# Decay matrices of a chunked gated DeltaNet: from masked triangle matmuls to cumulative sums spread by DMA, GpSimd adds and ScalarE exponentials

## The chip, the cores and the metric

One Trainium2 chip, one core. The metric is the device time of the whole kernel in microseconds (us), the median of several runs. A profiled execution has a span (first to last instruction) and a time of its own a little above it. Engines: PE is TensorE (PEld its weight loads), DVE is VectorE, ACT is ScalarE, POOL is GpSimd, SP is SyncE, which here only issues DMAs.

## The reference, cut to what matters

One layer over 512 latent tokens and 256 context tokens, width 2048: RMSNorm with adaLN, one combined input projection, a bidirectional gated DeltaNet (8 heads of 128), a grouped-query attention, gates, and output projections. Everything is float32. The change touches only the preparation of the DeltaNet, whose chunked form is:

```python
gcum = jnp.cumsum(gc, axis=-1)                       # log decays g <= 0, per token, head, direction
diff = gcum[..., :, None] - gcum[..., None, :]
decay_incl = where(incl, exp(diff), 0)               # incl: i >= j; strict: i > j
l_mat = (k*beta) @ k.T * decay_strict                # then (I + L)^-1 [v*beta, k*beta*exp(gcum)]
attn_intra = q @ k.T * decay_incl
q_dec, k_dec = q*exp(gcum), k*exp(gcum_last - gcum)
o = q_dec @ S + attn_intra @ v_new;  S = S*exp(gcum_last) + k_dec.T @ v_new
```

The kernel works with chunks of 128 tokens (the result doesn't depend on the chunk), so for each token tile, head and direction it needs a 128x128 matrix of decays.

## The kernel before, in words

**Weights.** Every big matmul is float32 made from three float32r products (`three`, L1675-1680): hi*hi, hi*lo, lo*hi. The weights come in 297 pieces of up to 128x1024 elements. For each piece SP loads `w_raw` (L561, two buffers), ACT rounds it to `w_hi` (`hi_part`, L766), DVE subtracts to get `w_lo` (`lo_part`, L1105), and PE multiplies. `w_hi` and `w_lo` have two buffers each. Each engine runs one loop over piece numbers n in program order. In iteration n, ACT first makes `w_hi` of piece n+1, which waits until PE has used piece n-1, and DVE first makes `w_lo` of piece n+1. So `w_lo` of piece n+1 has to be finished between the start and the end of PE's work on piece n.

**Slots.** The gate projections are pieces 121 to 216, of four k-tiles each. A k-tile is six 128x512 matmuls. Behind each k-tile PE, ACT and DVE run whatever `scan_plan` (L104) has put at that place, called a slot below; four slots make a piece. Slot number kk belongs to piece 122 + kk//4.

- Slots 0 to 119 prepare twelve *units* (L112-119). A unit is one token tile and one half of the heads (4 heads), both directions d. Units 0 to 3 are context tiles, at slots 0, 8, 16, 24; units 4 to 11 are latent tiles, at slots 32, 43, 54, 65, 76, 87, 98, 109. Relative to the unit's first slot: `kt` at +0, `decay` +1, `gram` +2, `qk` +3 (latent only), `lower` +5, `upper` +7, `at` +9 (latent only).
- From slot 126 the *scan* runs twelve pairs of units, each a chain of slots `couple5`, `ks`, `correct5`, `qs`, `couple6`, `correct6`, `z`, `az`, `kz`.
- The output of a gate group goes to DRAM in the first and the third slot of every fourth piece, with a Silu or Sigmoid on ACT (`gate_stage`, L1029). These need another table than the Exp of the `decay` slot.

**A unit, before.** `kt`: PE transposes four key blocks (L1693), ACT scales them into `k_rows` (L832, eight 128x128). `decay`: POOL has written masked copies of the log decays, high and low float32r parts (`decay_rhs`, L600, four 128x512); PE multiplies them by a triangle (L1702, L1703, two per direction); ACT takes Exp of PSUM into `decay` (`DD`, L842, one 128x512 per direction). `gram`: PE makes k.kT (L1710); DVE multiplies by a token factor and `decay` into `L` (L1215, eight 128x128). `lower` and `upper`: DVE copies out diagonal blocks (L1197, four 32x128 each, L1200 a transpose), and SP stores them (L518). `qk`: PE makes q.kT (L1715), DVE multiplies it into `decay` (L1225), POOL masks the result (`mask_scores`, L608). `at`: PE transposes that (L1721, eight), ACT copies it to `scoresT` (L848, two 128x512), SP stores it at +10 (L523).

**POOL** also inverts 32x32 diagonal blocks (`block_steps`, L627, L631), four steps of it in each latent unit, and loads and stores them by DMA. SP loads for the scan (L477, L485) after the last blocks are stored; the first scan matmul (L1760) waits for `L`.

Of the kernel before, what the change touches and what calls it, by code (L numbers as in the profile page):

```python
# [7 lines left out]
P = 128  # L8
# [11 lines left out]
NT = LT + CT  # L20
# [12 lines left out]
NCONST = SEL + 8  # L33

# [69 lines left out]
def scan_plan():  # L104
# [41 lines left out]
def build(nc, x, c, ctx, c_ctx, w_mod, b_mod, norm_w, w_in, conv_w, a_log, dt_bias, a_norm_w, q_norm_w,  # L146
# [80 lines left out]
    tri_r = [at(f"triangle{d}", [P, P], A_MASKS + 512 * d, f32r) for d in (0, 1)]  # L227
# [70 lines left out]
    GMH = [at(f"decay_rhs_hi{d}", [P, 4, P], A_C + 12288 + 2048 * d, f32r) for d in (0, 1)]  # L298
    GML = [at(f"decay_rhs_lo{d}", [P, 4, P], A_C + 16384 + 2048 * d, f32r) for d in (0, 1)]
    DD = [at(f"decay{d}", [P, 4, P], A_C + 20480 + 2048 * d) for d in (0, 1)]  # L300
# [11 lines left out]
    g_hi = at("g_hi", [P, NT * 16], A_T + 12288, f32r)  # L312
    g_lo = at("g_lo", [P, NT * 16], A_T + 12672, f32r)
# [48 lines left out]
    kr_scr = nc.dram_tensor("k_rows_scratch", [N_UNITS, P, 2, 512], f32, kind="Internal").ap()  # L362
    block_in = nc.dram_tensor("block_in_scratch", [N_UNITS, 8, P, 32], f32, kind="Internal").ap()
    block_out = nc.dram_tensor("block_out_scratch", [N_UNITS, 8, P, 32], f32, kind="Internal").ap()

    with ExitStack() as stack:
# [101 lines left out]
        def _(sp):  # L468
# [36 lines left out]
            def scan_transfers(kk):  # L505

                for u in UNITS:
# [67 lines left out]
        def _(pool):  # L575
# [13 lines left out]
            pool.wait_ge(S("prep"), 1)  # L589
            pool.wait_ge(S("w_used"), N_GATE0)  # L590
            def decay_rhs(u):
                for d in (0, 1):

                    col = unit_col(d, u["tile"], 4 * u["half"])
                    m = (GT, LT_)[d]
                    mask = consts[:, m:m + P].unsqueeze(1).to_broadcast([P, 4, P])
                    if u["i"]:
                        pool.wait_ge(S("decay_mm"), 2 * u["i"])
                    for part_t, g_t in ((GMH, g_hi), (GML, g_lo)):
                        ins = pool.tensor_tensor(part_t[d][:], mask,  # L600
                                                 g_t[:, col:col + 4].bitcast(f32).unsqueeze(2).to_broadcast([P, 4, P]), ALU.mult)
                    ins.then_inc(S("decay_rhs"), 1)

            def mask_scores(u):
                for d in (0, 1):
                    m = (GE, LE)[d]
                    pool.wait_ge(S("decayed"), 2 * u["li"] + d + 1)
                    pool.tensor_tensor(DD[d][:], DD[d][:], consts[:, m:m + P].unsqueeze(1).to_broadcast([P, 4, P]),  # L608
                                       ALU.mult).then_inc(S("masked"), 1)
# [31 lines left out]
            decay_rhs(UNITS[0])  # L641
            pool.memset(X64[:], 0.0).then_inc(S("zeroed"), 1)
            pool.wait_ge(S("kv_spill"), 16 * NT)
            pool.memset(SS[:], 0.0).then_inc(S("zeroed"), 1)
            for u in UNITS:
                if u["i"] + 1 < N_UNITS:
                    decay_rhs(UNITS[u["i"] + 1])
                if u["lat"]:
                    mask_scores(u)
                    if u["li"] == 0:  # L650
                        blocks_load(0)
                    block_steps(1 + 4 * u["li"], min(31, 5 + 4 * u["li"]))
            blocks_store(0)
            for d in (0, 1):
                pool.wait_ge(S("decay_mm"), 2 * N_UNITS)
# [94 lines left out]
        def _(act):  # L750
# [71 lines left out]
            def prepare(slot):  # L822
# [12 lines left out]
                elif k == "decay":  # L835
                    for d in (0, 1):
                        act.wait_ge(S("decay_mm"), 2 * i + d + 1)
                        if i:
                            act.wait_ge(S("L"), 2 * i)
                        if u["li"]:  # L840
                            act.wait_ge(S("scoresT_mm"), 2 * u["li"])
                        act.activation(DD[d][:], bank4(4 + 2 * d), ACT.Exp).then_inc(S("decay"), 1)  # L842
                elif k == "at":
                    for d in (0, 1):
                        act.wait_ge(S("scoresT_mm"), 2 * u["li"] + d + 1)
# [73 lines left out]
            for n in range(N_PA0):  # L919
# [62 lines left out]
                if n == GROUPS[G_BKV]["first"] + 5:  # L982

                    act.wait_ge(S("ab_rows"), 1)
                    ab = bank(6, NT * 32).rearrange("p (t c) -> p t c", t=NT)
                    act.activation(beta[:].rearrange("p (t c) -> p t c", t=NT), ab[:, :, 0:16], ACT.Sigmoid).then_inc(
                        S("beta"), 1)
                    act.wait_ge(S("negabs"), 1)
# [3 lines left out]
                    act.activation(alog[:], alog[:], ACT.Exp).then_inc(S("ab_exp"), 1)  # L992
                    act.wait_ge(S("ssq_eps"), 1)
                    ln(act.activation(rk[:], rk[:], ACT.Sqrt))
                    act.activation(rq[:], rq[:], ACT.Sqrt).then_inc(S("ssq_std"), 1)
                if n == GROUPS[G_BKV]["first"] + 6:
                    act.wait_ge(S("cum"), 1)
                    act.activation(DEC[:].rearrange("p a b c -> p (a b c)"), bank(6, NT * 2 * 24), ACT.Exp).then_inc(
                        S("decays"), 1)
                if n == N_GATE0:  # L1000
                    g = GROUPS[G_BKV]
                    for t in range(NT):
                        if t == 0:
# [88 lines left out]
        def _(dve):  # L1092
# [18 lines left out]
            for d, m in enumerate((LE, GE)):  # L1111
                dve.tensor_copy(tri_r[d][:], consts[:, m:m + P]).then_inc(S("triangles"), 1)
# [90 lines left out]
            def prepare(slot):  # L1203
# [31 lines left out]
            def scan(slot):  # L1235
# [5 lines left out]
                for d in (0, 1):  # L1241
# [44 lines left out]
                    elif k == "az":  # L1286
                        o = o_acc[:, tile, 4 * half * P:(4 * half + 4) * P].rearrange("p (u n) -> p u n", u=4)
                        dve.tensor_tensor(o, ps, o, ALU.add).then_inc(done, 1)
# [120 lines left out]
            for n in range(N_PA0):  # L1409
# [57 lines left out]
                if n == GROUPS[G_BKV]["first"] + 5:  # L1467
                    dve.wait_ge(S("ab_rows"), 1)
                    dve.wait_ge(S("beta"), 1)
# [7 lines left out]
                    dve.tensor_tensor(ab_t[1][:], ab_t[0][:], ab_t[1][:], ALU.min).then_inc(S("negabs"), 1)  # L1477
                    dve.wait_ge(S("ab_exp"), 1)
# [10 lines left out]
                    dve.scalar_tensor_tensor(out=v3(gdec), in0=v3(ab_t[0]), scalar=-1.0,  # L1489
                                             in1=alog[:].unsqueeze(1).to_broadcast([P, NT, 16]),  # L1490
                                             op0=ALU.mult, op1=ALU.mult).then_inc(S("g_ready"), 1)
# [3 lines left out]
                    dve.tensor_scalar(rq[:], bank(7, 32, 48), EPS, None, ALU.add).then_inc(S("ssq_eps"), 1)  # L1495
                    dve.wait_ge(S("ssq_std"), 1)
# [7 lines left out]
                if n == GROUPS[G_BKV]["first"] + 7:  # L1504
                    dve.wait_ge(S("decays"), 1)
                    ln(dve.tensor_scalar(ngr[:].rearrange("p (a h) -> p a h", h=8), DEC[:, :, 0, :], -1.0, None, ALU.mult))
                    ln(dve.tensor_tensor(v4(ngr), v4(ngr), rkb, ALU.mult))
                    ln(dve.tensor_copy(g_hi[:], gdec[:]))
# [543 lines left out]
```

## Time and profile before

| what | value |
|---|---|
| median of 3 runs | 1830.5 us (1828.3 to 1832.72) |
| profiled execution, own time | 1831.48 us |
| its span | 1828.9 us |
| PE busy | 1765.8 us, 97% |
| PEld busy | 1449.0 us, 79% |
| DVE busy | 946.3 us, 52% |
| ACT busy | 661.7 us, 36% |
| POOL busy | 277.3 us, 15% |
| mean granted TensorE clock | 0.993 |

The shares are over the whole span. The units' slots run from about 558 us to 765 us, the scan from 777 us to 1102 us. In the lines of the trace the first number is the start in us, the second the length, xN the number of instructions merged; square brackets give the idle time of that engine just before and what ended it.

### The profile page before, as it was taken

What the parts mean: (1) busy time and instruction counts of PE and PEld (TensorE: products, weight loads), DVE (VectorE), ACT (ScalarE), POOL (GpSimd) and SP (SyncE); (2) the same over time, 40 slices, a digit from 0 to 9 for tenths busy, and PEclk for the clock granted to TensorE, in tenths of its full rate; (3) what the DMA queues carried; (4) which work ended last, traced back from release to release, by engine and by line L of the source; (5) the groups of instructions that cost most, each with busy time, mean ns of one, the idle gap of its engine ahead of it and who ended that gap; (6) DMA issues with size and microseconds to landing.
All of it is one profiled execution on the core that took longest, in us unless ns stands there. A gap on an engine that the chain in (4) does not pass through costs nothing.

```text
span 1828.9 us, 25605 instructions
## 1 busy us (share of the span) xinstructions
PE 1765.8 (97%) x10286; PEld 1449.0 (79%) x10286; DVE 946.3 (52%) x1662; ACT 661.7 (36%) x1212; POOL 277.3 (15%) x421
## 2 busy tenths in 40 slices
PE   5899999999999999999999999999998999999999
PEld 3568888888787888788888888877877788788887
DVE  2335444365324575545556554764368866453334
ACT  5323321233135546444343435522346444232121
POOL 1000000000004466477000003211101110210000
PEclk9999999999999999999999999999999999999999
DMA  9982222223225666744444437767533333662332
GB/s 370 337 283 58 58 58 58 58 81 86 70 58 179 195 183 187 218 132 144 132 122 139 123 96 227 223 202 208 172 104 98 99 100 97 254 195 92 123 119 104
DMA packets 198685, 267.13 MB, mean 146 GB/s; under 512 B 37072, under 2 KB 135625, under 8 KB 197161
## 3 DMA queue, kind: packets, MB, share of 16 engines
q1 hardware_dynamic: 174944, 192.63, 34.8%
q0 software_dynamic: 15552, 58.62, 9.4%
q10 hardware_dynamic: 8073, 14.27, 2.1%
q8 instruction: 81, 1.33, 0.3%
q14 instruction: 35, 0.29, 0.0%
HBM read 221.96 MB, written 43.52 MB: 145 GB/s over the span
## 4 chain that ended last, share of the span: by engine, by line
PE 82%; DVE 7%; ACT 4%; DMA 4%; issue 2%; POOL 1%; SPq 0%; ACTq 0%; DVEq 0%; POOLq 0%
PE psum L1678 24%; PE psum L1680 23%; PE psum L1679 23%; DMA w_raw_mod<-w_mod_dram 2%; DVE w_lo L1105 1%; PE psum L1789 1%; PE psum L1787 1%; PE psum L1838 1%; PE psum L1671 1%; ACT w_hi L766 1%; PE psum L1793 1%; PE psum L1791 1%; PE psum L1795 1%; DMA w_raw<-w_proj_b_dram 1%; PE psum L2020 1%
## 5 line engine op out<-in xcount | busy, mean ns | idle before, releaser
L1105 DVE TENSOR_TENSOR w_lo<-w_raw,w_hi 128x1024 fp32r<-128x1024 f32 x232 | 290.7, 1253 | 538.9 <-ACT w_hi L766 538.5
L766 ACT ACTIVATE w_hi<-w_raw 128x1024 fp32r<-128x1024 f32 x232 | 245.7, 1059 | 834.2 <-PE psum L1680 776.5
L1678 PE MATMUL psum<-h_hi,w_hi 128*128 128x512 f32 x1152 | 470.7, 409 | 12.5 <-DVE hc_lo L1159 5.6
L1680 PE MATMUL psum<-h_hi,w_lo 128*128 128x512 f32 x1152 | 452.4, 393 | 0.0
L1679 PE MATMUL psum<-h_lo,w_hi 128*128 128x512 f32 x1152 | 451.9, 392 | 0.0
L1678 PEld LDWEIGHTS psum<-h_hi,w_hi 128*128 128x128 f32 x1152 | 217.5, 189 | 71.7 <-issue 23.9
L1680 PEld LDWEIGHTS psum<-h_hi,w_lo 128*128 128x128 f32 x1152 | 217.2, 189 | 48.8
L1679 PEld LDWEIGHTS psum<-h_lo,w_hi 128*128 128x128 f32 x1152 | 218.0, 189 | 36.5
L1174 DVE SCALAR_TENSOR_TENSOR conv_acc<-conv_in,convw,conv_acc 128x772 f32<-128x772 f32 x96 | 98.2, 1023 | 3.4
L1678 PE MATMUL psum<-w_hi,m_hi 128*128 128x512 f32 x256 | 99.6, 389 | 0.0
L1679 PE MATMUL psum<-w_lo,m_hi 128*128 128x512 f32 x256 | 99.6, 389 | 0.0
L1680 PE MATMUL psum<-w_hi,m_lo 128*128 128x512 f32 x256 | 99.6, 389 | 0.0
L600 POOL TENSOR_TENSOR decay_rhs_hi<-consts,g_hi 128x512 fp32r<-128x512 f32 x24 | 27.0, 1124 | 466.6 <-PE psum L1680 406.8
L1678 PE MATMUL psum<-w_hi,h_hi 128*128 128x512 f32 x192 | 75.4, 393 | 2.5 <-ACT gate_stage L1029 1.3
L1680 PE MATMUL psum<-w_hi,h_lo 128*128 128x512 f32 x192 | 74.8, 389 | 0.0
L1679 PE MATMUL psum<-w_lo,h_hi 128*128 128x512 f32 x192 | 74.7, 389 | 0.0
L1678 PE MATMUL psum<-hc_hi,w_hi 128*128 128x256 f32 x256 | 72.6, 283 | 0.0
L1679 PE MATMUL psum<-hc_lo,w_hi 128*128 128x256 f32 x256 | 72.3, 283 | 0.0
L1680 PE MATMUL psum<-hc_hi,w_lo 128*128 128x256 f32 x256 | 72.2, 282 | 0.0
L1678 PEld LDWEIGHTS psum<-w_hi,m_hi 128*128 128x128 f32 x256 | 48.1, 188 | 10.0
L1679 PEld LDWEIGHTS psum<-w_lo,m_hi 128*128 128x128 f32 x256 | 48.1, 188 | 10.0
L1680 PEld LDWEIGHTS psum<-w_hi,m_lo 128*128 128x128 f32 x256 | 48.1, 188 | 9.8
(323 smaller groups left out, 2831.7 us busy)
## 6 DMA issues: line engine op xcount, KB each, us to landing
w_raw<-w_in_dram SPq DMA_DIRECT2D x168, 512.0 KB, 4.0
w_raw_mod<-w_mod_dram SPq DMA_DIRECT2D x64, 512.0 KB, 6.0
w_raw_modg<-w_mod_dram POOLq DMA_DIRECT2D x32, 512.0 KB, 4.5
w_raw<-w_out_dram SPq DMA_DIRECT2D x32, 512.0 KB, 3.7
gate_scratch<-gate_stage ACTq DMA_DIRECT2D x48, 256.0 KB, 4.2
w_raw<-w_proj_a_dram SPq DMA_DIRECT2D x16, 512.0 KB, 4.0
w_raw<-w_proj_b_dram SPq DMA_DIRECT2D x16, 512.0 KB, 3.5
gates<-gate_scratch POOLq DMA_DIRECT2D x32, 256.0 KB, 4.0
```

What stands on the lines that cost most here:

```text
L600: ins = pool.tensor_tensor(part_t[d][:], mask, g_t[:, col:col + 4].bitcast(f32).unsqueeze(2).to_broadcast([P, 4, P]), ALU.mult)
L766: act.activation(part(whi[i % 2], p), part(place, p), ACT.Copy).then_inc(S("w_hi"), 1)
L1105: dve.tensor_tensor(part(wlo[i % 2], p), part(raw_of(n)[0], p), part(whi[i % 2], p).bitcast(f32), ALU.subtract).then_inc(S("w_lo"), 1)
L1174: ins = dve.scalar_tensor_tensor(out=a[:], in0=r[:, tap:tap + 772], scalar=w, in1=a[:], op0=ALU.mult, op1=ALU.add)
L1671: ins = pe.matmul(bank(7, 1, off + t * 8 + it["head"]), a[:, a0:a0 + P], ones[:, 0:1], start=True, stop=True)
L1678: pe.matmul(out_ap, lh, rh, start=first, stop=False, skip_group_check=shared)
L1679: pe.matmul(out_ap, lh, rl, start=False, stop=False, skip_group_check=shared)
L1680: return pe.matmul(out_ap, ll, rh, start=False, stop=last, skip_group_check=shared)
L1787: ins = pe.matmul(ps[:, u, :], kT_of(h, tile), SS[:, d, h, :], start=True, stop=True)
L1789: ins = pe.matmul(ps[:, u, :], YY[d][:, u, :], RR[d][:, u, :], start=True, stop=True)
L1791: ins = pe.matmul(ps[:, u, :], qT[:, h, tile * P:(tile + 1) * P], SS[:, d, h, :], start=True, stop=True)
L1793: ins = pe.matmul(ps[:, u, :], AT[:, d, u, :], ZZ[d][:, u, :], start=True, stop=True)
```

## The change

The decay matrices are no longer made by PE.

1. In the last piece before the gates (`prep`), PE makes cumulative sums of the log decays in two parts: DVE splits each log decay into a multiple of a quarter (adding and taking away `QUARTERS`) and a rest. The sum of the first part, `gdec`, is exact; the exponential of the sum of the rests is a token factor `alpha`. `gdec` is transposed by PE, copied to `cumT` and stored by POOL to DRAM.
2. For each unit POOL issues two DMAs (`cum_load`) that spread four rows of it to all 128 partitions (`CR`, two buffers), and adds a triangle of 0 and 1e30 (`beyond`) to them: `decay_args`, two 128x512 adds, and for latent units two 128x512 subtractions for the transposed matrix.
3. ACT takes Exp of them with the token's sum as bias: one instruction per head and direction, eight of 128x128 into `DD`, and for latent units eight more straight into `scoresT` (`AT`).
4. The scores are made transposed (k.qT), so DVE multiplies them straight into `scoresT` in the `qk` slot. The `at` slot, the mask on POOL and the PE transposes go. SP stores `scoresT` at +6.
5. `alpha` is folded into token factors; in `az` DVE uses it as a scalar: four 128x128 instructions per direction in place of one 128x512.
6. POOL's clearing of `states` moves behind the units.

```diff
-            for m, k in ((0, "kt"), (1, "decay"), (2, "gram"), (5, "lower"), (7, "upper"), (3, "qk"), (9, "at"))[:7 if lat else 5]:
+            for m, k in ((0, "kt"), (1, "decay"), (2, "gram"), (5, "lower"), (7, "upper"), (3, "qk"))[:6 if lat else 5]:
...
-                    if u["lat"] and kk == u["at"] + 10:
+                    if u["lat"] and kk == u["at"] + 6:
...
-            def decay_rhs(u):
...
-                    for part_t, g_t in ((GMH, g_hi), (GML, g_lo)):
-                        ins = pool.tensor_tensor(part_t[d][:], mask, ...)
-            def mask_scores(u):
...
+            def cum_load(u):
+                if u["i"] == 1:
+                    pool.wait_ge(S("kv_spill"), 16 * NT)
+                if u["i"] >= 2:
+                    pool.wait_ge(S("decay_args"), args_of[u["i"] - 2])
                 for d in (0, 1):
+                    r0 = unit_col(d, u["tile"], 4 * u["half"])
+                    pool.dma_start(CR[u["i"] % 2][:, d]..., cum_scr[r0:r0 + 4]....partition_broadcast(P)).then_inc(...)
+            def decay_args(u):
+                pool.wait_ge(S(f"cum_in{u['i'] % 2}"), 32 * (u["i"] // 2 + 1))
+                if u["i"]:
+                    pool.wait_ge(S("L"), 2 * u["i"])
                 for d in (0, 1):
+                    pool.tensor_tensor(DD[d][:], CR[u["i"] % 2][:, d], beyond[d]..., ALU.add).then_inc(S("decay_args"), 1)
+                if not u["lat"]:
+                    return
+                if u["li"]:
+                    pool.wait_ge(S("decayT"), 2 * u["li"])
+                for d in (0, 1):
+                    pool.tensor_tensor(DT[d][:], CR[u["i"] % 2][:, d], beyond[1 - d]..., ALU.subtract).then_inc(S("decay_args"), 1)
...
                 elif k == "decay":                                   # ACT
                     for d in (0, 1):
-                        act.wait_ge(S("decay_mm"), 2 * i + d + 1)
-                        act.activation(DD[d][:], bank4(4 + 2 * d), ACT.Exp).then_inc(S("decay"), 1)
-                elif k == "at":
-                        act.activation(AT[:, d], bank4(4 + 2 * d), ACT.Copy).then_inc(S("scoresT"), 1)
+                        act.wait_ge(S("decay_args"), first + d + 1)
+                        for w in range(4):
+                            ins = act.activation(DD[d][:, w, :], DD[d][:, w, :], ACT.Exp, scale=-1.0, bias=gdec[:, col:col + 1])
+                        ins.then_inc(S("decay"), 1)
+                    if not u["lat"]:
+                        return
                     for d in (0, 1):
+                        act.wait_ge(S("decay_args"), first + d + 3)
+                        if u["li"]:
+                            act.wait_ge(S("scores_out"), 16 * u["li"])
+                        for w in range(4):
+                            ins = act.activation(AT[:, d, w, :], DT[d][:, w, :], ACT.Exp, bias=cum_neg[:, col:col + 1])
+                        ins.then_inc(S("decayT"), 1)
...
-                        dve.wait_ge(S("L"), 2 * i + d + 1)
-                        dve.tensor_tensor(DD[d][:], bank4(7), DD[d][:], ALU.mult).then_inc(S("decayed"), 1)
+                        dve.wait_ge(S("decayT"), 2 * u["li"] + d + 1)
+                        dve.tensor_tensor(AT[:, d], bank4(4), AT[:, d], ALU.mult).then_inc(S("scoresT"), 1)
...
                     elif k == "az":
-                        dve.tensor_tensor(o, ps, o, ALU.add).then_inc(done, 1)
+                        for u in range(4):
+                            ins = dve.scalar_tensor_tensor(out=o, in0=ps[:, u, :], scalar=alpha[:, col:col + 1], in1=o,
+                                                           op0=ALU.mult, op1=ALU.add)
+                        ins.then_inc(done, 1)
...
-                elif k == "decay":                                   # PE
-                        pe.matmul(bank4(4 + 2 * d), tri_r[d][:], GMH[d][:], start=True, stop=False)
-                        pe.matmul(bank4(4 + 2 * d), tri_r[d][:], GML[d][:], start=False, stop=True).then_inc(S("decay_mm"), 1)
...
-                elif k == "at":
-                        for w in range(4):
-                            ins = pe.transpose(bank4(4 + 2 * d)[:, w, :], DD[d][:, w, :], ident)
...
                     for d in (0, 1):
+                        for v in (0, 1):
+                            pe.matmul(split[:, v, :, d, :], consts[:, (LE, GE)[d]:(LE, GE)[d] + P], part_logs, start=True, stop=True)
...
+                    pe.wait_ge(S("prep"), 4)
+                    pe.transpose(bank(7, P, 128)[0:NT * 16], gdec[:], ident).then_inc(S("prep_mm"), 1)
```

## Rows read from the trace of the kernel before

**Rows 1.** Windows: busy us (instructions) of each engine, clock, DMA share, GB/s.

```profile
560.00:760.00 200.00, 199.47 (x1006) 167.60 (x1005) 124.78 (x242) 104.85 (x189) 104.30 (x120) 1.00 0.61 184
```

**Rows 2.** Waits of PE, 500 to 800 us: in total, times, longest.

```profile
PE psum L1760 <- DMA L<-L_scratch: 3.7, 1, 3.7
PE psum L1678 <- ACT kv_stage L1007: 2.2, 1, 2.2
```

**Rows 3.** Timeline of PE in `prep` and in the decay and at slots.

```profile
538.95 1.43 PE L1951 MATMUL psum<-gdec,consts 128*128 128x48 f32 x12
...
559.64 0.39 PE L1702 MATMUL psum<-decay_rhs_hi,triangle 128*128 128x512 f32 x1
...
560.58 0.39 PE L1678 MATMUL psum<-h_hi,w_hi 128*128 128x512 f32 x1
...
626.19 1.03 PE L1721 MATMUL psum<-consts,decay 128*128 128x128 f32 x8
...
626.98 0.48 PE L1678 MATMUL psum<-h_hi,w_hi 128*128 128x512 f32 x1
```

**Rows 4.** Timeline of ACT in the scan: 128x128 instructions from SBUF.

```profile
816.63 2.45 ACT L878 ACTIVATE invT<-invT,beta 128x128 f32<-128x128 f32 x8 [4.24 <-DVE invT L1258]
```

**Rows 5.** Timeline of ACT around unit 8 (slots 76 to 86).

```profile
686.39 1.06 ACT L766 ACTIVATE w_hi<-w_raw 128x1024 fp32r<-128x1024 f32 x1 [0.81 <-PE psum L1680]
688.15 2.17 ACT L832 ACTIVATE k_rows<-psum,decays 128x128 f32<-128x128 f32 x8 [0.69 <-PE psum L1693]
...
693.99 1.08 ACT L842 ACTIVATE decay<-psum 128x512 f32<-128x512 f32 x2
...
697.44 1.06 ACT L766 ACTIVATE w_hi<-w_raw 128x1024 fp32r<-128x1024 f32 x1 [0.46 <-ACT gate_stage L1029]
700.52 1.06 ACT L766 ACTIVATE w_hi<-w_raw 128x1024 fp32r<-128x1024 f32 x1 [2.02 <-PE psum L1680]
```

**Rows 6.** Timeline of DVE around the same unit.

```profile
698.53 1.35 DVE L1105 TENSOR_TENSOR w_lo<-w_raw,w_hi 128x1024 fp32r<-128x1024 f32 x1 [0.51 <-ACT w_hi L766]
```

**Rows 7.** Timeline of ACT and DVE around unit 6 (slots 54 to 64).

```profile
644.21 1.06 ACT L766 ACTIVATE w_hi<-w_raw 128x1024 fp32r<-128x1024 f32 x1 [4.38 <-PE psum L1680]
...
654.05 1.06 ACT L766 ACTIVATE w_hi<-w_raw 128x1024 fp32r<-128x1024 f32 x1
659.25 1.06 ACT L766 ACTIVATE w_hi<-w_raw 128x1024 fp32r<-128x1024 f32 x1 [4.13 <-PE psum L1680]
...
655.15 2.00 DVE L1105 TENSOR_TENSOR w_lo<-w_raw,w_hi 128x1024 fp32r<-128x1024 f32 x1 [7.37 <-ACT w_hi L766]
657.07 2.15 DVE L1215 SCALAR_TENSOR_TENSOR L<-psum,crow,decay 128x128 f32<-128x128 f32 x8
660.34 3.54 DVE L1197 TENSOR_TENSOR L_diagonal<-L,consts 32x128 f32<-32x128 f32 x4
663.89 1.58 DVE L1105 TENSOR_TENSOR w_lo<-w_raw,w_hi 128x1024 fp32r<-128x1024 f32 x1
```

**Rows 8.** Timeline of DVE in a context unit.

```profile
579.94 1.17 DVE L1197 TENSOR_TENSOR L_diagonal<-L,consts 32x128 f32<-32x128 f32 x4
```

**Rows 9.** Lines of POOL, 545 to 766 us: busy, mean ns, idle before.

```profile
L600 POOL TENSOR_TENSOR decay_rhs_hi<-consts,g_hi 128x512 fp32r<-128x512 f32 x24 | 27.0, 1124 | 466.6 <-PE psum L1680 406.8 <-PE psum L1703 59.8
```

**Rows 10.** Last unit and start of the scan: SP, PE, and the clock there.

```profile
763.19 0.37 SPq L518 DMA_DIRECT2D block_in_scratch<-L_diagonal  x1
...
776.74 0.65 PE L1760 MATMUL psum<-inv32T,L 32*32 32x32 f32 x32 [3.70 <-DMA L<-L_scratch]
...
775.00:782.00 7.00, 5.26 (x48) 4.65 (x49) 1.15 (x5) 4.96 (x13) 5.98 (x14) 0.51 0.52 189
```

**Rows 11.** Timeline of DVE at an az slot of the scan.

```profile
899.04 1.43 DVE L1288 TENSOR_TENSOR o_acc<-psum,o_acc 128x512 f32<-128x512 f32 x2
902.05 2.16 DVE L1293 SCALAR_TENSOR_TENSOR states<-states,decays,psum 128x128 f32<-128x128 f32 x8 [1.58 <-PE psum L1795]
```

**Rows 12.** Timeline of POOL at the start of the units.

```profile
559.08 1.81 POOL L644 MEMSET states<- 128x2048 f32 x1 [4.99 <-DMA kv_scratch<-kv_stage]
```

More of the change, by code:

```diff
@@ L33 @@
 NCONST = SEL + 8
+QUARTERS = 1.5 * 2 ** 21
 def shape_constants():
@@ L225, in build @@
     consts = at("consts", [P, NCONST], A_CONST)
-    tri_r = [at(f"triangle{d}", [P, P], A_MASKS + 512 * d, f32r) for d in (0, 1)]
+    beyond = [at(f"beyond{d}", [P, P], A_MASKS + 512 * d) for d in (0, 1)]
     small_top = [A_SMALL]
@@ L297, in build @@
     KR = at("k_rows", [P, 2, 4, P], A_C + 8192)
-    GMH = [at(f"decay_rhs_hi{d}", [P, 4, P], A_C + 12288 + 2048 * d, f32r) for d in (0, 1)]
-    GML = [at(f"decay_rhs_lo{d}", [P, 4, P], A_C + 16384 + 2048 * d, f32r) for d in (0, 1)]
-    DD = [at(f"decay{d}", [P, 4, P], A_C + 20480 + 2048 * d) for d in (0, 1)]
+    DD = [at(f"decay{d}", [P, 4, P], A_C + 12288 + 2048 * d) for d in (0, 1)]
+    DT = [at(f"decayT{d}", [P, 4, P], A_C + 16384 + 2048 * d) for d in (0, 1)]
+    CR = [at(f"cum_rows{i}", [P, 2, 4, P], (A_C + 20480, A_T)[i]) for i in (0, 1)]
     DIAG = at("L_diagonal", [P, 2, 4, 32], A_C + 24576)
@@ L362, in build @@
     kr_scr = nc.dram_tensor("k_rows_scratch", [N_UNITS, P, 2, 512], f32, kind="Internal").ap()
+    cum_scr = nc.dram_tensor("cum_scratch", [NT * 16, P], f32, kind="Internal").ap()
     block_in = nc.dram_tensor("block_in_scratch", [N_UNITS, 8, P, 32], f32, kind="Internal").ap()
@@ L587, in _ @@
                 pool.memset(rawc[i][:], 0.0).then_inc(S("zeroed"), 1)
-            pool.wait_ge(S("prep"), 1)
+            pool.wait_ge(S("prep"), 6)
+            pool.dma_start(cum_scr, cumT[:]).then_inc(S("cum_out"), 16)
+            pool.wait_ge(S("cum_out"), 16)
             pool.wait_ge(S("w_used"), N_GATE0)
-            def decay_rhs(u):
-                for d in (0, 1):
[L594 to L598, printed above, removed]
-                    for part_t, g_t in ((GMH, g_hi), (GML, g_lo)):
-                        ins = pool.tensor_tensor(part_t[d][:], mask,
-                                                 g_t[:, col:col + 4].bitcast(f32).unsqueeze(2).to_broadcast([P, 4, P]), ALU.mult)
-                    ins.then_inc(S("decay_rhs"), 1)
@@ L604, in mask_scores @@
-            def mask_scores(u):
-                for d in (0, 1):
[L606 to L609, printed above, removed]
+            pool.wait_ge(S("beyond"), 2)
+            args_of = np.cumsum([4 if u["lat"] else 2 for u in UNITS]).tolist()
+            def cum_load(u):
[3 more added lines that the diff above has]
+                    pool.wait_ge(S("decay_args"), args_of[u["i"] - 2])
+                for d in (0, 1):
+                    r0 = unit_col(d, u["tile"], 4 * u["half"])
+                    pool.dma_start(CR[u["i"] % 2][:, d].rearrange("p u n -> p (u n)"),
+                                   cum_scr[r0:r0 + 4].rearrange("r n -> (r n)").partition_broadcast(P)).then_inc(
+                        S(f"cum_in{u['i'] % 2}"), 16)
@@ L1110, in _ @@
             dve.wait_ge(S("const_in"), 16)
-            for d, m in enumerate((LE, GE)):
-                dve.tensor_copy(tri_r[d][:], consts[:, m:m + P]).then_inc(S("triangles"), 1)
+            for d, m in enumerate((GE, LE)):
+                dve.tensor_scalar(beyond[d][:], consts[:, m:m + P], -1.0, -1e30, ALU.add, ALU.mult).then_inc(S("beyond"), 1)
             dve.wait_ge(S("rowsT"), 1)
@@ L1712, in prepare @@
                 elif k == "qk":
-                    pe.wait_ge(S("k_rows"), i + 1)
+                    if li:
+                        pe.wait_ge(S("scoresT"), 2 * li)
                     for w, h in enumerate(heads):
-                        ins = pe.matmul(bank4(7)[:, w, :], qT[:, h, tile * P:(tile + 1) * P], kT_of(h, tile), start=True, stop=True)
+                        ins = pe.matmul(bank4(4)[:, w, :], kT_of(h, tile), qT[:, h, tile * P:(tile + 1) * P], start=True, stop=True)
                     ins.then_inc(S("qk_mm"), 1)
-                elif k == "at":
-                    for d in (0, 1):
-                        pe.wait_ge(S("masked"), 2 * li + d + 1)
-                        for w in range(4):
-                            ins = pe.transpose(bank4(4 + 2 * d)[:, w, :], DD[d][:, w, :], ident)
-                        ins.then_inc(S("scoresT_mm"), 1)
             def scan(slot):
```

116 lines of the change are left out of this document (65 added, 51 removed).

## The prediction

> **What bounds the kernel now.** I read the windows of the stretch that holds the twelve units first. PE is busy 199.5 of 200 us there, at full clock, while DVE, ACT and POOL are busy a little over half of it [rows 1]. The list of PE's waits then names only two of more than half a microsecond between 500 and 800 us: 2.2 us for `kv_stage` and 3.7 us for `L` at the start of the scan [rows 2]. So PE sets the time, and work taken off it is worth its full length as long as the others keep up. Last I read the timelines of ACT and DVE around single units, because a half-busy engine that runs its queue in order can still be late at one place. The place to watch is `w_lo`: ACT's `w_hi` of a piece stands in its queue behind the unit's exponentials, and DVE's `w_lo` behind ACT's `w_hi`. When ACT starts the next `w_hi` after a wait for PE, that start shows, 0.25 us late, when PE began a piece.
>
> Around unit 8 ACT runs without a real pause from 686.4 to 698.5 us: `w_hi`, `k_rows`, table, gate output, table, exponentials, table, gate output, `w_hi` [rows 5]. DVE finishes that piece's `w_lo` at 699.88 [rows 6]. PE starts the piece at about 700.52 - 0.25 = 700.3 [rows 5]. The slack is 0.4 us. Around unit 6 it is 659.0 - 657.15 = 1.85 us, and for the piece after that DVE is busy with L, the scores and a slow `L_diagonal` until `w_lo` ends at 665.47 [rows 7]; PE wants it one piece and an at slot after 659.0, at 665.3. Hence little is free there, though the busy shares say half.
>
> **What PE loses.** From the start of a decay slot's matmuls to the next projection matmul: 560.58 - 559.64 = 0.94 us [rows 3], twelve times, 11.3 us. An at slot: 626.98 - 626.19 = 0.79, and 0.09 more because the matmul behind it lasts 0.48 and not 0.39 [rows 3]: 0.88 us, eight times, 7.0 us. Together 18.3 us. Score matmuls stay as many with their operands exchanged.
>
> **What PE gains in work.** Four more small float32 products, recorded as eight, at 1.43/12 = 0.12 us each [rows 3]: 1.0 us. The one transpose falls after piece 120, where PE waits 2.2 us for `kv_stage` anyway [rows 2]: nothing; without that cover 0.1 to 0.4 us.
>
> **What ACT gains in work.** Two Exp of 128x512, 1.08 us together [rows 5], become sixteen of 128x128. The trace has no such Exp. The nearest rows are `k_rows`, eight of that size from PSUM with a pointer as scale in 2.17 us [rows 5], and `invT`, eight of that size from SBUF to SBUF, also with a pointer, in 2.45 us [rows 4]. The latter means 0.39 us for the first and 0.295 for each further one, so sixteen take 4.8 us; by the former they take 4.2. I take 4.8, since the new ones read SBUF. ACT's queue between `k_rows` and the next `w_hi` grows by 4.8 - 1.1 = 3.7 us per latent unit (3.1 at the other end) and by 1.4 per context unit. The copies of the at slot (1.1 us) go, but stand elsewhere in the queue. The sixteen of unit 8 are followed in the queue by a gate output, then by `w_hi`.
>
> The Trainium skill ("ScalarE: Activation LUTs", section "What ACT_TABLE_LOAD costs") says that an ACTIVATE costs the same for every function, with a fixed part to which a pointer operand adds, and that back-to-back ones overlap in part; by its figures sixteen would be an estimated 4.8 us whatever they read. That speaks against the cheaper row, and with the cheaper row the sum below would be about 3.5 us less; no row here shows an Exp of this size.
>
> **Does PE wait for it?** PE's deadlines come 0.94 us sooner too (no decay slot). I worked out each unit: a piece is 5.44 us (two `w_hi` that both wait for PE are 1.06 + 4.38 apart [rows 7]), plus 0.44 for a kt slot (half an at slot) and 0.88 for each of gram and qk (eight instructions, like at); ACT and DVE in queue order with the lengths of the rows.
> - Context units: ACT's pause before `w_hi` is longer than 1.4 us. Nothing. Unit 4: 0.1 us.
> - Unit 8: `w_lo` ends 3.7 us later, at 703.6, and PE wants it at 700.3 - 0.9 = 699.4. Wait about 4.4 us.
> - Unit 6: `w_lo` starts 3.7 later, and with 1.35 (as behind unit 8 [rows 6]) instead of 2.00 ends at 660.2; wanted at 659.0 - 0.9 = 658.1: 2.1 us. Unit 10 has the same place in its piece, and 0.9 us of delay left from unit 9: 0.9 + 1.3. Unit 5: 1.4. Unit 7: 1.3. Unit 9: the queue has room, 0.
>   Together 11.5 us from `w_hi` being late. PE waits 0.5 us of this kind now (the third of its waits, left out of the rows), which I take off: 11.0.
> - Second round. In units 6 and 10 DVE's L waits behind that late `w_lo`, then come L and the scores (657.07 to 660.34 now), `L_diagonal` 3.5, and only then the next `w_lo` 1.6 [rows 7]. PE waits again, 3.0 and 2.9 us. After unit 7: 0.8. Together 6.7 us. The bounds: `L_diagonal` takes 3.54 us in unit 6 and 1.17 in a context unit [rows 7, 8], where POOL is idle. POOL's work hardly shrinks: four 128x512 and two masks become four 128x512, at about 1.1 us each [rows 9], and they start as soon as L is done, so I keep the slow value. With the quick one this whole term goes.
> - Clock. After the 3.7 us wait at the scan's start the granted clock is 0.51 for 7 us [rows 10], the 1.2 GHz level; PE's 5.3 busy us there are worth about half. After unit 8's 4.4 us I expect the same, 2.9 us. After waits of 3 us it may or may not come; I count none and keep 2.9 each for the upper end.
>
> **The end of the units.** Unit 11 too has its exponentials between two gate outputs. `w_lo` and the scores behind it are 3.2 us later, but the mask on POOL that ran beside the last `L_diagonal` is gone. So the last block store, 763.19 now, comes 1.4 to 4 us later relative to the unit, and the scan starts a fixed 13.5 us after it [rows 10]; PE's own progress doesn't matter there, it arrives early either way. I take 2.8 us, and nothing is gained for unit 11's decay and at slots.
>
> **What costs nothing.** In az DVE takes 2.16 us instead of 1.43, like any eight 128x128 [rows 11]; it is idle 1.58 us before the next slot's work, which it waits for from PE. If that cover were gone: 0.7 us for each of six pairs. The first spread: the store of the sums can't start before 549; even with two transfers of 6 us POOL has data by 561, and it must wait for the `kv` store until 559.1 in any case [rows 12]. Adds and exponentials end by 565, where `w_hi` is due at 564: hidden by the half piece of room behind it; at worst 1 to 3 us. The 24 spreads of 256 KB add 6 MB to 184 GB/s over 200 us [rows 1], 17% more; loads are issued a piece ahead, so nothing.
>
> **The sum.** Gained up to unit 11: 11 x 0.94 + 7 x 0.88 = 16.5. Lost: 11.0 + 6.7 + 2.9 + 1.0 + 2.8 = 24.4. Net +7.9 us. The profiled execution took 1831.5 us (span 1828.9 and 2.6 around it), 1.0 above the median of the runs; applied to the median, the forecast is 1838 us.
>
> **Rivals.**
> - *Balance.* The `w_hi` waits come, but the second round and the clock don't, because POOL and DVE meet less. -16.5 + 11.0 + 1.0 + 2.8 = -1.7: 1829 us. For it: spans of DVE instructions vary with what runs beside them [rows 7, 8]. Against: the adds start right at L's end.
> - *Faster.* PE keeps its whole gain, -18.3 + 1.0 = -17.3: 1813 us. This needs the exponentials to be hidden, at unit 8 within 0.4 us of slack less 0.9 of earlier deadline, so sixteen in about 1 us; or else only some units late. For it: ACT is busy only 105 of 200 us [rows 1], and a few late pieces of eight units could be all. Half of my first-round waits and nothing else would give about 1821.
> - *Starved.* The spreads or the store of the sums delay weight loads, a microsecond for each of thirty pieces: 1860 us. Against: a DMA share of 0.61 [rows 1].
>
> **How the numbers follow.** A difference of 0.2%, 3.7 us, is about what a measurement of this kernel can tell from no change. Forecast 0.50 (1834 to 1847: 1838 with up to three more clock drops); balance 0.22; faster 0.24; starved 0.04. Slower is 0.54, same 0.22, faster 0.24. The low end: by the cheaper exponentials (-3.5), no second round (-6.7) and no clock loss (-2.9) 1838 becomes 1825; the faster case reaches further, so I set 1819, with half of it below. High end 1847.
>
> **What would show it.** Right: Exp groups of sixteen lasting 4.5 us or more; PE waiting for `w_lo` some ten times between 600 and 765 us, 15 to 20 us in total, the longest behind unit 8 with a clock near 0.5 after it; ACT's wait for PE before `w_hi` much shorter. The number of PE instructions falls by 112, less 8 and 1. Wrong: PE still 99% busy there, or `w_lo` on time behind the exponentials; `L_diagonal` back at 1.2 us would take away the second round; waits for `cum_rows` or `w_raw` would mean the last rival.

## The result, and the profile after

The changed kernel takes 1836.7 us, the median of 22 runs (1830.0 to 1841.6); the kernel before, in the same sessions, 1830.1 (22 runs). The ratio is 1.0035, 95% interval 1.0026 to 1.0043: slower by 4.8 to 7.9 us. The profiled execution is one of the quicker: 1832.07 us, span 1830.1.

The page of the kernel after, busy us and instructions of each engine:

```profile
PE 1752.9 (96%) x10183; PEld 1436.4 (78%) x10183; DVE 963.6 (53%) x1717; ACT 687.8 (38%) x1333; POOL 280.6 (15%) x422
```

PE lost 103 recorded instructions (112 less 8 and 1, as forecast) and 12.9 us of busy time, and yet the kernel isn't faster. The windows of the same 200 us as in [rows 1] say where it went, and two smaller ones show the granted clock (the column behind POOL's):

```profile
560.00:760.00 200.00, 184.52 (x880) 151.95 (x880) 129.45 (x236) 128.59 (x305) 112.75 (x129) 0.97 0.69 211
...
653.00:661.00 8.00, 7.02 (x24) 5.30 (x22) 7.95 (x14) 2.63 (x4) 6.13 (x6) 0.79 0.81 263
...
700.00:707.00 7.00, 6.73 (x20) 5.40 (x21) 6.87 (x11) 0.00 (x0) 6.14 (x10) 0.64 0.71 225
```

PE is busy 184.5 of 200 us instead of 199.5, although part of that is at the lower clock. The small windows mix two levels: in windows of 2 us the clock is 0.50, the 1.2 GHz level, from 702 to 704 us and 1.00 from 706 to 708. PE's waits from 500 to 800 us (in total, times, longest), to set beside [rows 2]:

```profile
PE psum L1722 <- DVE w_lo L1132: 18.5, 10, 4.3
PE psum L1722 <- ACT kv_stage L1034: 2.1, 1, 2.1
PE psum L1786 <- DMA L<-L_scratch: 1.0, 1, 1.0
```

Ten waits for `w_lo` where there was one of 0.5 us. ACT's timeline around unit 8, the piece of [rows 5]:

```profile
690.37 2.46 ACT L863 ACTIVATE decay<-decay,gdec 128x128 f32<-128x128 f32 x8
692.74 2.44 ACT L873 ACTIVATE scoresT<-decayT,cum_neg 128x128 f32<-128x128 f32 x8
695.19 1.28 ACT L1056 ACT_TABLE_LOAD   x1
696.49 0.60 ACT L1056 ACTIVATE gate_stage<-psum 128x512 f32<-128x512 f32 x1
...
697.54 2.00 ACT L788 ACTIVATE w_hi<-w_raw 128x1024 fp32r<-128x1024 f32 x2 [0.46 <-ACT gate_stage L1056]
```

The sixteen exponentials take 4.8 us, from 690.37 to 695.18, where two took 1.08. ACT then makes two `w_hi` at once, without a wait for PE between them (before there were 2.02 us of it): it is late, not PE. PE starts that piece at 700.27, after 4.31 us. DVE around unit 6, the place of [rows 7]:

```profile
651.34 1.23 DVE L1132 TENSOR_TENSOR w_lo<-w_raw,w_hi 128x1024 fp32r<-128x1024 f32 x1 [8.18 <-ACT w_hi L788]
...
655.75 4.37 DVE L1224 TENSOR_TENSOR L_diagonal<-L,consts 32x128 f32<-32x128 f32 x4
660.13 1.48 DVE L1132 TENSOR_TENSOR w_lo<-w_raw,w_hi 128x1024 fp32r<-128x1024 f32 x1
```

and POOL beside it:

```profile
654.79 2.57 POOL L620 TENSOR_TENSOR decay<-cum_rows,beyond 128x512 f32<-128x512 f32 x2 [11.81 <-DVE L L1242]
657.33 2.64 POOL L627 TENSOR_TENSOR decayT<-cum_rows,beyond 128x512 f32<-128x512 f32 x2
```

DVE had waited 8.18 us for the first `w_hi`; PE lost 1.96 us there. Then `L_diagonal` takes 4.37 us, while POOL's adds run beside it, and PE waits another 1.65 us for the second `w_lo`: the second round.

Unit 9 has a wait of the second round too, which is easily taken for one of the first. ACT's `w_hi` was done at 723.27, but DVE got to its `w_lo` only behind a slow `L_diagonal` (and the upper blocks), and PE waited 1.15 us, until 728.42:

```profile
720.43 3.96 DVE L1224 TENSOR_TENSOR L_diagonal<-L,consts 32x128 f32<-32x128 f32 x4
...
727.15 1.22 DVE L1132 TENSOR_TENSOR w_lo<-w_raw,w_hi 128x1024 fp32r<-128x1024 f32 x1
```

Sorted by what stood before the late `w_lo`, six of the ten waits are of the first round, 11.8 us (0.98, 1.96, 0.98, 4.31, 0.49 and 3.05 in units 5, 6, 7, 8, 10 and 11), and four of the second, 6.8 us (1.65, 0.65, 1.15 and 3.31 in units 6, 7, 9 and 10).

At the end of the units DVE finishes the last diagonal block at 770.3 instead of 763, and the scan starts at 781.1 instead of 776.7, with 1.0 us of waiting instead of 3.7. The kernel before loses some 3 us more behind its start, at a clock of 0.51 [rows 10]; the kernel after doesn't. The two profiled executions were already apart in front of the units. This is the end of PE's wait for `kv_stage`, in the kernel before and in the kernel after, and the scan's start in the kernel after:

```profile
550.83 0.50 PE L1678 MATMUL psum<-h_hi,w_hi 128*128 128x512 f32 x1 [2.18 <-ACT kv_stage L1007]
```

```profile
549.57 0.50 PE L1722 MATMUL psum<-h_hi,w_hi 128*128 128x512 f32 x1 [2.07 <-ACT kv_stage L1034]
...
781.13 0.45 PE L1786 MATMUL psum<-inv32T,L 32*32 32x32 f32 x32 [0.99 <-DMA L<-L_scratch]
```

Call the time between the two *the stretch of the units*: 225.9 us before [rows 10], 231.6 after, so 5.7 us longer. Behind the scan's start the execution is 3.2 us shorter, and in front it is 1.3 us ahead, although `prep` has more work: a difference between two executions, not of the change. 5.7 - 3.2 - 1.3 = 1.2, by which the span grew.

### The profile page after: what moved, and what is told of

Read it like the earlier page. It is cut to its first block, busy times and chain, and to the rows that moved or that the text cites. A ratio compares the mean times of both kernels' runs of the same rounds, so it can differ in the third digit from the quotient of the medians.

```text
span 1830.1 us, 25534 instructions
## 1 busy us (share of the span) xinstructions
PE 1752.9 (96%) x10183; PEld 1436.4 (78%) x10183; DVE 963.6 (53%) x1717; ACT 687.8 (38%) x1333; POOL 280.6 (15%) x422
## 4 chain that ended last, share of the span: by engine, by line
PE 80%; DVE 7%; ACT 6%; DMA 3%; issue 2%; POOL 1%; ACTq 0%; SPq 0%; DVEq 0%; POOLq 0%
PE psum L1722 24%; PE psum L1723 23%; PE psum L1724 23%; DVE w_lo L1132 2%; PE psum L1864 1%; PE psum L1815 1%; ACT w_hi L788 1%; PE psum L1813 1%; DMA w_raw_mod<-w_mod_dram 1%; PE psum L1715 1%; PE psum L2053 1%; PE psum L1821 1%; PE psum L1817 1%; ACT scoresT L873 1%; DMA w_raw<-w_proj_b_dram 1%
## 5 line engine op out<-in xcount | busy, mean ns | idle before, releaser
L646 POOL TENSOR_TENSOR inv_outer<-inv_blocks 128x30 f32<-128x30 f32 (+14 forms) x90 | 55.0, 611 | 18.1 <-DMA inv_blocks<-block_in_scratch 11.8
```

The costliest lines, as they stand in the source:

```text
L646: pool.tensor_tensor(outer, BL[:, k + 1:32, k:k + 1].to_broadcast([P, 31 - k, k]), BL[:, k:k + 1, 0:k].to_broadcast([P, 31 - k, k]), ALU.m ...
```

## The experiments

The theories. *Queue*: the small exponentials make ACT's in-order queue late, `w_hi` and `w_lo` stand behind them, PE waits. *POOL*: POOL's adds beside `L_diagonal` slow DVE down, which makes a second wait. *Saving*: PE's removed matmuls were not worth their length. *az*: DVE's additional instructions in the scan cost time. Ratios are to the kernel before, run in the same session; a difference between two experiments is that of their ratios times 1829 us. The ratios' intervals reach 1.6 to 3.1 us to either side, so such a difference is uncertain by some 2 to 4 us.

**e1: half of the exponentials later.**

```diff
-  (2, "gram"), (5, "lower"), (7, "upper"), (3, "qk"))[:6 if lat else 5]
+  (2, "gram"), (5, "lower"), (7, "upper"), (5, "decayT"), (8, "qk"))[:7 if lat else 5]
...
-  if u["lat"] and kk == u["at"] + 6:      # store of scoresT
+  if u["lat"] and kk == u["at"] + 10:
```

> The kernel after, with the eight transposed exponentials of a latent unit moved from the decay slot (+1) to a new slot at +5, the score matmuls and their multiplication from +3 to +8, and the store of scoresT from +6 to +10. The work of every engine is the same. Theory 1 (ACT's in-order queue: w_hi stands behind 4.8 us of exponentials, so w_lo is late and PE waits): each w_hi is now delayed by 2.4 us less. The ten waits of PE for w_lo, 18.5 us now, fall to about 3 (unit 8's 4.3 to 1.9, the rest 1 at most), and the clock stays up: about 1820 us, at most 1826. Rival A (the second round and POOL are most of it): half of the waits stay, 1828. Rival B (PE's saved matmuls never were worth their length): no change beyond 0.2%, 1837.

1814.3 us, ratio 0.9919 (0.9907 to 0.9932): 21 us less than the kernel after, with the same work. PE's waits:

```profile
PE psum L1722 <- DVE w_lo L1132: 7.8, 5, 2.8
...
PE psum L1786 <- DVE states L1324: 0.4, 1, 0.4
```

ACT around unit 8 in e1:

```profile
689.38 1.28 ACT L1056 ACT_TABLE_LOAD   x1
690.67 0.60 ACT L1056 ACTIVATE gate_stage<-psum 128x512 f32<-128x512 f32 x1
691.30 0.33 ACTq L1059 DMA_DIRECT2D gate_scratch<-gate_stage  x1
691.73 1.06 ACT L788 ACTIVATE w_hi<-w_raw 128x1024 fp32r<-128x1024 f32 x1 [0.46 <-PE psum L1724]
692.80 1.28 ACT L873 ACT_TABLE_LOAD   x1
694.10 2.45 ACT L873 ACTIVATE scoresT<-decayT,cum_neg 128x128 f32<-128x128 f32 x8
```

One `w_hi` now goes between the two halves. The *queue* is the main cause, and *saving* falls as a cause: 1837 is far off. (The edit moves DVE's score multiplication too; e2 and e7 leave it where it was.) I had expected 1820 and 3 us of waits left; the waits left are 7.8, so the additional gain came from elsewhere: the clock is 1.00 in all 40 us windows from 560 to 800 us but one (0.96), where the kernel after has 0.96, 0.91, 0.96 and 0.96 in the last four, some 7 us of full speed, and the scan starts without the wait for `L`.

**e2: four exponentials instead of sixteen.**

```diff
-  for w in range(4):
...
-      ins = act.activation(DD[d][:, w, :], DD[d][:, w, :], ACT.Exp, scale=-1.0, bias=gdec[:, col:col + 1])
+  ins = act.activation(DD[d][:], DD[d][:], ACT.Exp, scale=-1e-30)
```

and the same for `AT` from `DT`, with `scale=1e-30`.

> The kernel after, with one Exp of 128x512 per direction in place of four of 128x128 with a bias (4 instead of 16 in a latent unit). It leaves out the bias, so the decays are not those of the reference; PE, DVE, POOL and the DMAs do the same work. Theory 1 (fixed cost of small instructions on ACT): four take 2.2 us instead of 4.8, the waits for w_lo fall from 18.5 to about 3 us in total, about 1819 us. If bytes and not instructions set ACT's time, four take 4 us or more and the time stays near 1835. Rival A (second round from POOL): waits of 5 to 6 us stay, 1825.

1822.0 us, ratio 0.9964 (0.9950 to 0.9979): 13 us less than the kernel after. The same bytes take 2.2 us instead of 4.8 (unit 8: 1.15 and 1.14 for two each), so the cost is one of instructions, not of bytes (with the bias column, which each of the sixteen had and these four don't; its share isn't separated). But four waits of together 8.5 us are left, nearer to rival A than to theory 1. Two of them, 2.71 and 2.96 us, are the second round of units 6 and 10; there the first round is gone. DVE and PE in unit 10 of e2:

```profile
734.15 4.39 DVE L1220 TENSOR_TENSOR L_diagonal<-L,consts 32x128 f32<-32x128 f32 x4
738.56 1.38 DVE L1128 TENSOR_TENSOR w_lo<-w_raw,w_hi 128x1024 fp32r<-128x1024 f32 x1
```

```profile
740.08 0.76 PE L1718 MATMUL psum<-h_hi,w_hi 128*128 128x512 f32 x1 [2.96 <-DVE w_lo L1128]
```

So the second round isn't merely an echo of a late `w_lo`: it comes by itself, where a slow `L_diagonal` stands before a `w_lo`.

**e3: POOL's adds later.**

```diff
-  pool.wait_ge(S("L"), 2 * u["i"])
+  pool.wait_ge(S("diagonal"), u["i"])
```

> The kernel after, with POOL's adds of a unit waiting until DVE has cut out the diagonal blocks of the unit before (slot +7) instead of until its L is made. ACT's and PE's queues are unchanged. Theory 2 (POOL's adds beside L_diagonal slow it and make the second round): L_diagonal takes about 1.2 us for four instead of 3.5 to 4.4, the second-round waits (1.65, 0.65, 3.31 us) go, the first-round ones stay: 5 us less than the kernel after, 1831 us. Rival A (L_diagonal is slow for another reason, or L's lateness alone makes the second round): the time stays, 1837. Rival B (the adds now end too late and the exponentials wait for POOL): slower, 1840 or more.

1824.9 us, ratio 0.9979 (0.9967 to 0.9990): 10 us less than the kernel after. `L_diagonal` on DVE, first in the kernel after, then in e3 (busy us, mean ns; from 560 to 765 us, which leaves two of the 48 of the kernel after outside):

```profile
L1224 DVE TENSOR_TENSOR L_diagonal<-L,consts 32x128 f32<-32x128 f32 x46 | 36.2, 787 | 4.7 <-DMA block_in_scratch<-L_diagonal 4.3
```

```profile
L1224 DVE TENSOR_TENSOR L_diagonal<-L,consts 32x128 f32<-32x128 f32 x48 | 13.5, 281 | 0.9 <-DMA block_in_scratch<-L_diagonal 0.4
```

2.8 times as fast, every one at the 0.28 us of a context unit [rows 8]. All four second-round waits are gone (1.65, 0.65, 1.15 and 3.31 us); those of the first round stay, 12.7 us in all against 11.8, unit 8's at 4.18. *POOL* is the cause of the second round. The edit moves POOL's inversion steps away from `L_diagonal` together with the adds, and the steps slow it as well: in unit 8 of the kernel after it took 2.82 us for four beside steps alone. It gave 10 us and not 5: PE's waits fell by 5.8, the granted clock of the four stretches from 640 to 800 us rose from 0.96, 0.91, 0.96, 0.96 to 1.00, 0.96, 0.96, 1.00, about 5 us of full speed.

**e4 and e7: the exponentials alone, in the kernel before.**

```diff
-  act.activation(DD[d][:], bank4(4 + 2 * d), ACT.Exp).then_inc(S("decay"), 1)
+  for w in range(4):
+      ins = act.activation(DD[d][:, w, :], bank4(4 + 2 * d)[:, w, :], ACT.Exp, bias=...)
+  if u["lat"]:
+      for w in range(4):
+          ins = act.activation(bank4(4 + 2 * d)[:, w, :], bank4(4 + 2 * d)[:, w, :], ACT.Exp, bias=...)
+  ins.then_inc(S("decay"), 1)
```

This is e7's edit. In e4 the additional eight stand in front of the others, write into `scoresT`, and wait for its store.

> The kernel before, with one part of the change alone: the exponentials in pieces of 128x128 with a pointer operand, eight in a context unit and sixteen in a latent one (the second eight write copies into scoresT, which the at slot overwrites). They read PSUM. PE keeps its decay and at slots. Theory 1: ACT's queue grows by 3.1 to 3.7 us before w_hi in latent units, PE's deadlines stay where they were, so PE waits for w_lo behind units 5 to 8, 10 and 11, some 10 to 14 us in total, and with the clock and the later end of the units the time is about 1843 us (1838 to 1848), that is slower than the kernel after, because nothing is saved. Rival (ACT's length doesn't matter, the loss of the changed kernel comes from POOL, DMAs or the operands' exchange): within 0.2% of 1830.

1860.6 us, ratio 1.0171 (1.0157 to 1.0185). The bias column held ones in all partitions but the first, so its decays are about e times too large; the number and shapes of the instructions are those meant. This run doesn't answer the question, because ACT in front of the exponentials of unit 10 looks like this:

```profile
751.96 1.28 ACT L846 ACT_TABLE_LOAD   x1 [5.90 <-DMA scoresT_scratch<-scoresT]
```

The additional eight wait for the store of the unit before, issued only at +10: five waits, 19.3 us in all. e7 is without them.

> e4 without its flaw (there the second eight waited for the store of scoresT, 14 us in all, which the changed kernel's do not): the kernel before with 128x128 exponentials, the second eight of a latent unit written over their own PSUM source, the bias a column of zeros. At 0.25 us each ACT's queue grows by 3.0 us in a latent unit, PE's deadlines stay. Theory 1: waits for w_lo of 7 to 10 us, most behind units 8, 10 and 11, plus 1 to 3 us of clock: 1838 us (1834 to 1843). Rival (ACT's length alone costs nothing): 1828.4, within 0.2%.

1842.4 us, ratio 1.0066 (1.0054 to 1.0078): 12 us slower, with 8.8 us of waits for `w_lo` (0.5 before), in six places, and 4.2 for `L` (3.7 before). e4 is 19 us slower still, so a wait put ahead of `w_hi` is as dear as work put there. Its sixteen take 4.2 us (697.59 to 701.81). PE behind unit 8, and the clock after that:

```profile
707.27 0.50 PE L1683 MATMUL psum<-h_hi,w_hi 128*128 128x512 f32 x1 [3.24 <-DVE w_lo L1110]
```

```profile
707.00:715.00 8.00, 7.73 (x31) 6.32 (x32) 7.04 (x11) 1.08 (x2) 5.02 (x8) 0.79 0.47 133
```

The stretch of the units is 13.0 us longer than before. The exponentials alone make a kernel slower whose PE work hasn't changed: the *queue* is shown from the other side too.

**e5: e1 and e3 together.**

> The edits of e1 and e3 together: transposed exponentials at +5, scores at +8, and POOL's adds behind the diagonal blocks of the unit before. If the two causes are separate places, they add up: of the five waits that e1 left (7.8 us) the two behind DVE's slow L_diagonal (1.2 and 1.9 us) go, those at the gate outputs of units 8 and 11 (2.8 and 1.6 us) stay: 1811 us. If e1 had already taken away all that POOL costs, the time stays at 1814. If the later adds make the exponentials wait, 1818 or more.

1813.5 us, ratio 0.9911 (0.9897 to 0.9924). Against e1 1.5 us, within the intervals: the times alone can tell the 3 us expected neither from nothing nor from 1.5. In the trace both causes are where they were expected: of e1's five waits the three behind `L_diagonal` (1.17, 1.92 and 0.33) are gone (`L_diagonal` at 281 ns), 4.9 us are left in three places, 2.51 of them behind unit 8, and the stretch of the units is 211.5 us instead of e1's 215.4.

**e6 and e10: both gate outputs at once.**

```diff
-  if q in (0, 2) and n and ... and n - 1 == GROUPS[pg]["last"]:
-      j = q // 2
+  ends = q == 0 and n and ... and n - 1 == GROUPS[pg]["last"]
+  for j in (0, 1) if ends else ():
```

> e5 with both gate outputs of a group taken one after the other in the first slot (before: first and third slot). The unit's exponentials then don't stand between them, and ACT loads a table once less. The longest wait left, 2.8 us behind unit 8, falls by one table load and the gate output, to about 0.5 us, and unit 11's 1.6 us goes: 1808 us, about what PE's own work gives (1828.4 - 17.3 for the instructions saved - 4.2 for the two waits that before has = 1807). If something else than ACT's queue holds up w_lo there, no change against e5.

1808.9 us, ratio 0.9892 (0.9875 to 0.9909). ACT around unit 8 in e6:

```profile
681.28 0.60 ACT L1056 ACTIVATE gate_stage<-psum 128x512 f32<-128x512 f32 x1
681.91 0.33 ACTq L1059 DMA_DIRECT2D gate_scratch<-gate_stage  x1
682.28 0.60 ACT L1056 ACTIVATE gate_stage<-psum 128x512 f32<-128x512 f32 x1 [0.40 <-ACT gate_stage L1056]
682.91 0.33 ACTq L1059 DMA_DIRECT2D gate_scratch<-gate_stage  x1
683.27 1.28 ACT L863 ACT_TABLE_LOAD   x1 [0.39 <-ACT gate_stage L1056]
684.56 2.45 ACT L863 ACTIVATE decay<-decay,gdec 128x128 f32<-128x128 f32 x8
686.92 1.05 ACT L788 ACTIVATE w_hi<-w_raw 128x1024 fp32r<-128x1024 f32 x1
```

The wait behind unit 8 is 1.13 us, the longest 1.20. This is the best version: 20 us faster than the kernel before. e10 is the same edit on the kernel after, alone.

> The kernel after with both outputs of a gate group in the first slot and nothing else changed: where a unit's exponentials stood between the two outputs (units 5, 8, 11) ACT loads a table once less and the second output no longer stands between the exponentials and w_hi. ACT's queue theory: the wait behind unit 8 falls from 4.3 us to about 3, unit 11's from 3.05 to about 1.7, the rest as in the kernel after: about 1833.5. If the position of the gate outputs were the main cause of the loss: 1828 or less. If ACT's lateness there isn't from the table loads: 1836.7.

1828.9 us, ratio 0.9991 (0.9979 to 1.0004): 8 us less than the kernel after, more than the 3 expected and near the 1828 of the rival that makes the place of the gate outputs the main cause. The waits speak against that rival, as 13.1 us of them are left. Unit 8's wait is 2.85 us and unit 11's 0.57, as forecast (3 and 1.7) or better; all waits for `w_lo` fall from 18.5 us by 5.4. The rest fits the clock, whose mean over the runs is 0.991 here and 0.9885 in the kernel after; no run separates it.

**e8: az as it was.**

> The kernel after with az as it was: one 128x512 addition per direction, so alpha is left out of that product. The prediction put az at nothing, since DVE is idle 1.58 us there. Then the time is that of the kernel after, 1836.7. If az's 0.7 us for each of six pairs is on the path: 1832.5.

1836.7 us, ratio 1.0038 (1.0023 to 1.0053), the same as the kernel after. *az* costs nothing, though DVE's az work rose from 10.9 to 17.3 us there.

**e9: the saved work put back.**

```diff
...
+  elif k == "decay":
+      for again in range(4):
+          pe.matmul(bank(6), h_hi[:, 0, 0:P], h_hi[:, 0, :], start=True, stop=True)
+  elif k == "upper" and un["lat"]:
+      for again in range(8):
+          pe.transpose(bank4(6)[:, again % 4, :], consts[:, 0:P], ident)
```

> e6 with the work that the change saved put back on PE alone, its results used by nobody: four 128x512 float32r matmuls in each decay slot and eight 128x128 transposes in the upper slot of each latent unit. ACT, DVE, POOL and SP do what they do in e6. The prediction counts 12 x 0.94 + 8 x 0.88 = 18.3 us for it. If PE's saving is worth its full length once nobody is late: e6's 1808.9 + 18.3, less the waits of e6 that the longer deadlines take up (2.8 for w_lo), so 1824 to 1827. If the saving was worth much less than counted: under 1818.

1826.0 us, ratio 0.9975 (0.9965 to 0.9985): 15.2 us more than e6, 18.3 less the 2.8 us of waits that vanish (the trace of e9 has none left for `w_lo`) being 15.5. The traces say it more closely than the medians: the stretch of the units is 222.2 us in e9 and 207.8 in e6, 14.4 more, and 18.3 less those 2.8 and e6's wait of 1.2 for `L`, which e9 hasn't either, is 14.3. PE's saving is worth its full length, as soon as nobody is late.

## Why the prediction was right

1838 was forecast, with slower as the likeliest; 1836.7 was measured. The mechanism came as forecast, in two rounds and with the clock; that the number is within 1.3 us is in part luck, as the sum below shows. Step by step:

- **PE's saving**, 18.3 us: right, by e6 and e9. That work off PE is worth its length "as long as the others keep up" was the condition, and it failed in the kernel after.
- **Sixteen exponentials in 4.8 us**: measured 4.8 in every latent unit, the value of the row from SBUF [rows 4]. From PSUM sixteen took 4.2 us in e7, as the other row said [rows 5]. The estimate by the Trainium skill ("ScalarE: Activation LUTs", "What ACT_TABLE_LOAD costs") is 4.8 as well and agrees for SBUF; the prediction took it to hold "whatever they read", which e7 doesn't bear out.
- **First round**, 11.5 us: measured 11.8. Forecast and measured for each unit: unit 4 0.1 and 0, unit 5 1.4 and 0.98, unit 6 2.1 and 1.96, unit 7 1.3 and 0.98, unit 8 4.4 and 4.31, unit 9 0 and 0, unit 10 2.2 and 0.49, unit 11 none and 3.05. Unit 10's is small because PE had lost 1.15 us just before, in unit 9's second round; without that wait, in e3, it is 1.93. Unit 11 was the miss: I held that PE's own progress doesn't matter there, and put all of its loss into the end of the units. So the total is right by two errors against each other.
- **Second round**, 6.7 us: measured 6.8. Forecast and measured: unit 6 3.0 and 1.65, unit 7 0.8 and 0.65, unit 9 none and 1.15, unit 10 2.9 and 3.31. e3 shows that POOL is its cause, which was argued from two rows only.
- **Clock**, 2.9 us, and "after waits of 3 us it may or may not come": the granted clock falls around the waits of 1.96, 4.31, 3.31 and 3.05 us (8.5 us of full speed in the windows of the profiled run, some of it while PE was waiting anyway), and before's own fall at the scan's start, 3.4, is gone. Net 5.1, in size between the one that I counted and the three more that I left to the upper end. I had counted no loss at unit 6, and hadn't seen that before's own would go. The 2.9 itself is an estimate above its row, whose 5.3 busy us at 0.51 lose 2.6.
- **End of the units**, 2.8 us: the premise failed. The scan doesn't start a fixed 13.5 us after the last block store: it is 10.8 us in the kernel after (770.36 to 781.13) and 12.5 in e3 (760.10 to 772.61). The store comes 7.2 us later, the scan only 4.4, and the clock loss that the kernel before has behind it is gone. I hadn't seen that a late scan start takes away a loss that the kernel before has.
- **az, the first spread, the DMAs**: nothing, as forecast. e8 shows the first; no wait for `w_raw` among PE's and none for `cum_rows` among POOL's show the others.
- The rivals: *balance* didn't come, as both the second round and the clock losses did. *Faster* needed the exponentials hidden; e1, e5 and e6 are that case, at 1814 to 1809. *Starved* has no sign.

For the stretch of the units in the profiled executions the sum is -18.3 for PE's work, +18.0 for the waits for `w_lo`, -2.7 for the wait for `L` and +8.5 for the clock: 5.5, where 5.7 was measured and the forecast comes to 6.9 (7.9 less the 1.0 of `prep`). The agreement is good to a microsecond or so, since part of the 8.5 passed while PE waited. Behind the scan's start the forecast has nothing, and 3.2 us were gained. With `prep` that makes a growth of 3.5 us, where 7.9 was forecast and the medians differ by 6.6. The 3 us between 3.5 and 6.6 are not in the mechanism as forecast: the profiled run of the kernel after was one of its quicker ones. The mean granted clock over a run was 0.990 in that run and 0.9885 on average of 22, against 0.993 and about 0.992 before; 0.0035 of 1830 us is 6 us. Why the clock differs between runs of the same kernel stays open.

## What to carry over

Work taken off the engine that sets the time is worth its full length only if what replaces it fits into the in-order queues ahead of that engine's next operand; look at the one deadline in each period (here `w_hi`, then `w_lo`), not at busy shares. If it doesn't fit, cut the replacement into parts around that deadline: the same instructions in two slots instead of one turned 7 us of loss into 15 us of gain. Count small instructions by their number, and keep POOL's adds away from the stretch in which DVE's work on SBUF operands is urgent.

## What the runs showed that I had not expected

- With POOL's adds and inversion steps beside them, DVE's 32x128 instructions on two SBUF operands (`L_diagonal`) take 0.79 us on average instead of 0.28 (e3). The score multiplication, which reads one operand from PSUM, isn't slowed: two of 128x512 take 1.28 us beside the adds in unit 6 of the kernel after (654.55) and 1.28 with POOL idle in e3 (656.45).
- The clock's answer isn't the same each time: in e3 it shows 0.79 over 8 us after waits of 4.18 and of 3.18 us, but 1.00 after 2.02 and 1.93; in the kernel after it fell after 1.96. The windows of e3 around the ends of its waits of 4.18 (until 697.28) and 1.93 us (until 732.90), each with a part of the wait:

```profile
695.00:703.00 8.00, 5.72 (x18) 4.57 (x19) 4.82 (x11) 1.91 (x2) 3.01 (x2) 0.79 0.64 212
730.00:738.00 8.00, 6.07 (x27) 4.71 (x26) 6.33 (x16) 2.53 (x5) 0.16 (x1) 1.00 0.47 143
```
